# A hybrid decoder block on one core: the down projection's matmuls in two of 256 tokens

## The chip, the cores and the metric

The kernel runs on one core of a Trainium2 chip. The metric is the device time of one execution, in microseconds. Before the change two runs gave 2263.14 and 2269.77 us, median 2266.45 us.

## The reference, cut to what matters

One layer of a decoder on 512 tokens, model width 2048: a projection into three mixers (a state-space scan, a sparse attention and a short convolution), an output projection, and a gated MLP of width 5632. The change touches only the last product of the last lines, `@ ffn_w_down`:

```
h  = rmsnorm(x, norm_mix);  proj = h @ w_in
x  = x + concat[ssd(...), dsa(...), shortconv(...)] @ w_out
h2 = rmsnorm(x, norm_ffn)
g  = causal_dwconv(h2 @ ffn_w_gate, ffn_conv_w)      # 2048 -> 5632, 3 taps along the tokens
x  = x + (silu(g) * (h2 @ ffn_w_up)) @ ffn_w_down    # 5632 -> 2048
```

All is float32 at the interface. Inside, each operand of a large product is split in two, a rounded high part (type fp32r) and the rest as low part (fp32r too), and a product is made of three matmuls: high x high, low weights x high, high weights x low.

## The kernel before, in words

Everything is kept transposed: channels on the 128 partitions, the 512 tokens along the free axis. A weight tile is 128 x 128, a matmul takes it as its stationary operand (`whi` or `wlo`) and streams a 128 x 512 activation block (`hhi`, `yhi`, `ahi` or their low parts) into one bank of the accumulator memory, `ps`, which holds 512 float32 a partition.

Stages in time: the w_in projection with the mixers' work laid between its matmuls (to some 660 us), w_out (to some 825 us), then the MLP in 4 chunks of 11 feature tiles (1408 of the 5632 features). In a chunk, the gate and up projections fill `ahi`/`alo` (11 blocks of 128 x 512), and then the down projection, `down(ch)`, runs over the 16 output tiles: a hardware loop of 8 iterations with 2 output tiles each. One output tile contracts over the chunk's 11 feature tiles, in four quarters of 3, 3, 3 and 2 tiles (`DOWN_K`); its matmuls all add into one of two banks, and VectorE adds that bank to the residual (L1204).

The weights go through a chain of four engines, a quarter at a time: SyncE loads it from memory into one of 4 `raw` slots (L345), ScalarE rounds it into one of 8 `whi` slots (L636), GpSimd subtracts to get `wlo` (L376) and counts `lo_ready`, and TensorE waits for `lo_ready` at the head of the quarter (L400), runs the quarter's matmuls, and counts `w_used` with the last, which frees the slots. A tile's first quarter also waits until VectorE has read the bank, and each quarter waits for `a_lo`, the activations' low parts, which are early but for the last block in a chunk's first tile.

`quarter` is the function that issues a quarter's matmuls, for every projection: three a feature tile, lines 406, 407 and 408. For each matmul instruction that it issues, the trace shows two on TensorE, LDWEIGHTS (the engine PEld) and MATMUL (the engine PE). Down has 4 chunks x 16 output tiles x 11 feature tiles x 3 = 2112 matmuls. TensorE's other, smaller matmuls belong to the mixers (helper `side`); they are of plain float32, for which the trace shows two MATMULs an instruction, with a LDWEIGHTS each.

Of the kernel before, what the change touches and what calls it, by code (L numbers as in the profile page):

```python
# [29 lines left out]
T = 512  # L30
# [127 lines left out]
def hybrid_block(nc, xT, w_in, w_out, w_gu, w_dn, params, relb, cmats, onehot, bias_rows, acs_rows, out):  # L158
# [4 lines left out]
    with ExitStack() as ctx:  # L163
        def sb(name, shape, dt=F32):
            return ctx.enter_context(nc.sbuf_tensor(name, shape, dt))
# [9 lines left out]
        whi = sb("whi", [P, NW, T], F32R)  # L175
        wlo = sb("wlo", [P, NW, T], F32R)
# [93 lines left out]
        def bank(i):  # L270
            return ps[:, i, :]
# [67 lines left out]
        @block.sync  # L339
        def _(sp_):  # L340
            def load(slot, n, src, width):

                if not isinstance(n, int) or n >= NRAW:
                    sp_.wait_ge(lo_ready, n - NRAW + 1)
                sp_.dma_start(raw[:, slot % NRAW, 0:width], src).then_inc(raw_loaded[slot % NRAW], 16)  # L345


            for n in range(8):
                load(n, n, w_in[n % 2, :, n // 2 * T:(n // 2 + 1) * T], T)
                for i in {0: (0,), 1: (1,), 3: (2, 3), 5: (4, 5)}.get(n, ()):  # L350
                    load_x(sp_, i)
            load_x(sp_, 6)
            load_x(sp_, 7)
            with sp_.Fori(2, NPROJ) as t:
                for q in range(4):
                    load(q, 4 * t + q, w_in[bass.ds(t, 1), :, q * T:(q + 1) * T].rearrange("a p n -> (a p) n"), T)
            with sp_.Fori(0, KT) as t:
                for q in range(4):
                    load(q, 4 * t + (QN_OUT + q), w_out[bass.ds(t, 1), :, q * T:(q + 1) * T].rearrange("a p n -> (a p) n"), T)
            with sp_.Fori(0, FCH) as c:  # L360
                with sp_.Fori(0, 2 * FPC) as f:
                    for q in range(4):
                        load(q, QN_CHUNK * c + 4 * f + (QN_FFN + q),
                             w_gu[bass.ds(2 * FPC * c + f, 1), :, q * T:(q + 1) * T].rearrange("a p n -> (a p) n"), T)
                with sp_.Fori(0, KT) as d:
                    for q, (k0, kn) in enumerate(DOWN_K):
                        load(q, QN_CHUNK * c + 4 * d + (QN_FFN + 8 * FPC + q),
                             w_dn[bass.ds(KT * c + d, 1), :, k0 * P:(k0 + kn) * P].rearrange("a p n -> (a p) n"), kn * P)
# [26 lines left out]

        @block.tensor
        def _(pe):
            def quarter(slot, n, dst, src_hi, src_lo, ks, first, last, before=None):

                pe.wait_ge(lo_ready, n + 1)  # L400
                for i, k in enumerate(ks):
                    if before is not None:
                        before(k)
                    w = slice(i * P, (i + 1) * P)
                    s = slot % NW
                    nc.tensor.matmul(dst, whi[:, s, w], src_hi[:, k, :], start=first and i == 0, stop=False)  # L406
                    nc.tensor.matmul(dst, wlo[:, s, w], src_hi[:, k, :], start=False, stop=False)  # L407
                    ins = nc.tensor.matmul(dst, whi[:, s, w], src_lo[:, k, :], start=False,  # L408
                                           stop=last and i == len(ks) - 1)
                ins.then_inc(w_used, 1)  # L410
# [149 lines left out]
            for n in range(8):  # L560

                if n >= 4:
                    side(1, n - 4)
                quarter(n, n, acc(n % 2), hhi, hlo, range(4 * (n // 2), 4 * (n // 2) + 4), n < 2, n >= 6,
                        (lambda k: pe.wait_ge(h_lo, k + 1)) if n % 2 == 0 else None)
            for t in range(2, NPROJ):
                for q in range(4):
                    side(t, q)
                    if q == 0 and t >= 4:
                        wait_read(pe, t - 2)  # L570
                    quarter(4 * t + q, 4 * t + q, acc(t), hhi, hlo, range(4 * q, 4 * q + 4), q == 0, q == 3)


            for c in range(2):
                wait_read(pe, TN_OUT + c - 2)
                for q in range(4):
                    n = QN_OUT + 4 * c + q
                    quarter(n, n, bank((TN_OUT + c) % 2), yhi, ylo, range(4 * q, 4 * q + 4), q == 0, q == 3,
                            (lambda k: pe.wait_ge(y_lo, k + 1)) if c == 0 else None)
# [23 lines left out]
            def down(ch):  # L603
                with pe.Fori(0, KT // 2) as d:
                    for c in range(2):
                        pe.wait_ge(acc_read[(TN_FFN + c) % 2],
                                   (TN_CHUNK // 2) * ch + d + (TN_FFN + 2 * FPC + c - 2) // 2 + 1)
                        for q, (k0, kn) in enumerate(DOWN_K):

                            pe.wait_ge(a_lo, FPC * ch + (FPC if q == 3 else FPC - 1))  # L610
                            n = QN_FFN + 8 * FPC + 4 * c + q
                            quarter(n, QN_CHUNK * ch + 8 * d + n, bank((TN_FFN + c) % 2), ahi, alo,
                                    range(k0, k0 + kn), q == 0, q == 3)

            with pe.Fori(1, FPC) as f:
                for c in range(2):
                    gate_or_up(c, 8 * f, f)
            down(0)
            with pe.Fori(1, FCH) as ch:
                with pe.Fori(0, FPC) as f:  # L620
                    for c in range(2):
                        gate_or_up(c, QN_CHUNK * ch + 8 * f, (TN_CHUNK // 2) * ch + f)
                down(ch)
# [677 lines left out]
```

## Time and profile before

| | |
|---|---|
| runs shown | 2263.14 and 2269.77 us, median 2266.45 us |
| profiled execution | span 2264.7 us; the page gives no other time of it |
| TensorE matmuls (PE) | 2248.7 us busy (99%), 10196 |
| TensorE weight loads (PEld) | 1832.2 us busy (81%), 10196 |
| VectorE | 810.5 us (36%) |
| ScalarE | 754.0 us (33%) |
| GpSimd | 1076.2 us (48%) |
| DMA | mean 100 GB/s |

Busy time is time in which the engine had at least one instruction under way. A matmul's record lasts longer than the distance to the next one's, since they are pipelined, so a busy PE says little: the pace is read from the starts. The granted clock is given as a share of full speed, 1.00 for 2.4 GHz and 0.50 for 1.2 GHz.

### The profile page before, as it was taken

What the parts mean: (1) busy time and instruction counts of PE and PEld (TensorE: products, weight loads), DVE (VectorE), ACT (ScalarE), POOL (GpSimd) and SP (SyncE); (2) the same over time, 40 slices, a digit from 0 to 9 for tenths busy, and PEclk for the clock granted to TensorE, in tenths of its full rate; (3) what the DMA queues carried; (4) which work ended last, traced back from release to release, by engine and by line L of the source; (5) the groups of instructions that cost most, each with busy time, mean ns of one, the idle gap of its engine ahead of it and who ended that gap; (6) DMA issues with size and microseconds to landing.
All of it is one profiled execution on the core that took longest, in us unless ns stands there. A gap on an engine that the chain in (4) does not pass through costs nothing.

```text
span 2264.7 us, 32528 instructions
## 1 busy us (share of the span) xinstructions
PE 2248.7 (99%) x10196; PEld 1832.2 (81%) x10196; DVE 810.5 (36%) x1170; ACT 754.0 (33%) x1287; POOL 1076.2 (48%) x872
## 2 busy tenths in 40 slices
PE   8999999999999999999999999999999999999999
PEld 6777778887888888888888888888888888888887
DVE  5489565777651223222002233102233101332200
ACT  6343334443343334433222222222222222222221
POOL 4445334545464445444554444455444455444453
PEclk9999999999999999999999999999999999999999
DMA  5323122333252223222332222333222233222243
GB/s 185 87 81 117 63 70 86 121 96 99 83 186 96 96 82 111 94 96 85 96 112 94 99 96 89 91 96 109 97 97 97 80 98 110 96 97 93 86 132 97
DMA packets 132696, 226.18 MB, mean 100 GB/s; under 512 B 14728, under 2 KB 48968, under 8 KB 132648
## 3 DMA queue, kind: packets, MB, share of 16 engines
q1 hardware_dynamic: 126144, 210.82, 29.0%
q10 hardware_dynamic: 6504, 14.73, 2.0%
q8 instruction: 29, 0.48, 0.1%
q14 instruction: 19, 0.16, 0.0%
HBM read 220.74 MB, written 4.62 MB: 100 GB/s over the span
## 4 chain that ended last, share of the span: by engine, by line
PE 91%; DVE 6%; issue 1%; DMA 1%; ACT 1%; SPq 0%; ACTq 0%; DVEq 0%
PE ps L406 30%; PE ps L408 29%; PE ps L407 29%; DVE work L993 1%; DVE work L992 1%; DVE work L896 1%; PE ps L502 0%; PE ps L488 0%; DVE work L895 0%; DVE work L923 0%; PE ps L474 0%; DMA cm<-cmats 0%; DVE work L984 0%; PE ps L543 0%; DVE work L971 0%
## 5 line engine op out<-in xcount | busy, mean ns | idle before, releaser
L376 POOL TENSOR_TENSOR wlo<-raw,whi 128x512 fp32r<-128x512 f32 (+1 forms) x868 | 1076.0, 1246 | 1171.2 <-ACT whi L636 1170.3
L406 PE MATMUL ps<-hhi,whi 128*128 128x512 f32 x2192 | 867.8, 396 | 2.7 <-DVE hlo L1133 2.7
L408 PE MATMUL ps<-hlo,whi 128*128 128x512 f32 x2192 | 855.9, 390 | 0.0
L407 PE MATMUL ps<-hhi,wlo 128*128 128x512 f32 x2192 | 855.3, 390 | 0.0
L636 ACT ACTIVATE whi<-raw 128x512 fp32r<-128x512 f32 (+1 forms) x868 | 504.4, 589 | 931.6 <-PE ps L408 886.2
L406 PEld LDWEIGHTS ps<-hhi,whi 128*128 128x128 f32 x2192 | 412.7, 188 | 105.3 <-issue 17.9
L408 PEld LDWEIGHTS ps<-hlo,whi 128*128 128x128 f32 x2192 | 412.5, 188 | 87.2
L407 PEld LDWEIGHTS ps<-hhi,wlo 128*128 128x128 f32 x2192 | 413.0, 188 | 85.7 <-issue 2.4
L406 PE MATMUL ps<-ahi,whi 128*128 128x512 f32 x704 | 274.0, 389 | 0.0
L407 PE MATMUL ps<-ahi,wlo 128*128 128x512 f32 x704 | 274.0, 389 | 0.0
L408 PE MATMUL ps<-alo,whi 128*128 128x512 f32 x704 | 273.9, 389 | 0.0
L1204 DVE TENSOR_TENSOR resid<-ps,resid 128x512 f32 x64 | 44.3, 692 | 424.1 <-PE ps L408 424.1
L407 PEld LDWEIGHTS ps<-ahi,wlo 128*128 128x128 f32 x704 | 132.2, 188 | 27.5
L406 PEld LDWEIGHTS ps<-ahi,whi 128*128 128x128 f32 x704 | 132.2, 188 | 27.4
L408 PEld LDWEIGHTS ps<-alo,whi 128*128 128x128 f32 x704 | 132.2, 188 | 27.3
L1194 DVE TENSOR_TENSOR upv<-ps,rstd 128x512 f32<-128x512 f32 x44 | 30.4, 691 | 295.0 <-PE ps L408 295.0
L1185 DVE TENSOR_TENSOR gpad<-ps,rstd 128x512 f32<-128x512 f32 x44 | 30.5, 692 | 294.7 <-PE ps L408 294.2
L407 PE MATMUL ps<-yhi,wlo 128*128 128x512 f32 x256 | 99.6, 389 | 0.0
L408 PE MATMUL ps<-ylo,whi 128*128 128x512 f32 x256 | 99.6, 389 | 0.0
L406 PE MATMUL ps<-yhi,whi 128*128 128x512 f32 x256 | 99.6, 389 | 0.0
L836 ACT ACTIVATE gsilu<-gconv 128x512 f32<-128x512 f32 x44 | 27.8, 632 | 139.6 <-DVE gconv L1189 139.6
L1197 DVE TENSOR_TENSOR act<-upv,gsilu 128x512 f32<-128x512 f32 x44 | 69.0, 1569 | 8.7 <-DVE upv L1194 8.7
(171 smaller groups left out, 1215.0 us busy)
## 6 DMA issues: line engine op xcount, KB each, us to landing
raw<-w_gu SPq DMA_DIRECT2D x352, 256.0 KB, 3.1
raw<-w_in SPq DMA_DIRECT2D x196, 256.0 KB, 3.2
raw<-w_dn SPq DMA_DIRECT2D x192, 192.0 KB, 2.3
raw<-w_out SPq DMA_DIRECT2D x64, 256.0 KB, 3.1
raw<-w_dn SPq DMA_DIRECT2D x64, 128.0 KB, 2.2
resid<-xT SPq DMA_DIRECT2D x8, 512.0 KB, 7.1
work<-acs_rows ACTq DMA_DIRECT2D x8, 512.0 KB, 3.9
resid<-xT ACTq DMA_DIRECT2D x8, 512.0 KB, 7.2
```

What stands on the lines that cost most here:

```text
L376: nc.gpsimd.tensor_tensor(wlo[:, slot % NW, 0:width], raw[:, slot % NRAW, 0:width], whi[:, slot % NW, 0:width].bitcast(F32), ALU.subtract) ...
L406: nc.tensor.matmul(dst, whi[:, s, w], src_hi[:, k, :], start=first and i == 0, stop=False)
L407: nc.tensor.matmul(dst, wlo[:, s, w], src_hi[:, k, :], start=False, stop=False)
L408: ins = nc.tensor.matmul(dst, whi[:, s, w], src_lo[:, k, :], start=False, stop=last and i == len(ks) - 1)
L636: A(whi[:, slot % NW, 0:width], raw[:, slot % NRAW, 0:width], ACT.Copy).then_inc(hi_ready, 1)
L836: A(gsilu[:, :], gconv[:, :], ACT.Silu).then_inc(f_silu, 1)
L896: ch_.link(V.scalar_tensor_tensor(r, t, 1.5, r, ALU.add, ALU.mult))
L992: ch_.link(V.max(top8, score[b]))
L1185: V.tensor_tensor(gpad[:, 2:], bank(TN_FFN % 2), rstd2[:, :], ALU.mult).then_inc(acc_read[TN_FFN % 2], 1)
L1194: V.tensor_tensor(upv[:, :], bank(par1), rstd2[:, :], ALU.mult).then_inc(acc_read[par1], 1)
L1197: V.tensor_tensor(act[:, :], upv[:, :], gsilu[:, :], ALU.mult).then_inc(f_act, 1)
L1204: V.tensor_tensor(blk(resid, 2 * d + p), bank((TN_FFN + p) % 2), blk(resid, 2 * d + p), ALU.add).then_inc(acc_read[(TN_FFN + p) % 2], 1)
```

## The change

`quarter` gets a flag, `halves`, which is set in `down` alone. With it, each matmul of 128 x 512 becomes two of 128 x 256, with the same weights, one directly behind the other: tokens 0 to 255 and tokens 256 to 511, into the two halves of the same bank. The flag that starts the bank's sum anew stands at the first half of the tile's first matmul alone. The count `w_used` goes with the last half.

```diff
-            def quarter(slot, n, dst, src_hi, src_lo, ks, first, last, before=None):
+            def quarter(slot, n, dst, src_hi, src_lo, ks, first, last, before=None, halves=False):
...
                     s = slot % NW
+                    if halves:
+                        for weight, src in ((whi, src_hi), (wlo, src_hi), (whi, src_lo)):
+                            for h in range(2):
+                                cols = slice(h * T // 2, (h + 1) * T // 2)
+                                ins = nc.tensor.matmul(dst[:, cols], weight[:, s, w], src[:, k, cols],
+                                                       start=first and i == 0 and weight is whi and src is src_hi and h == 0,
+                                                       stop=last and i == len(ks) - 1 and src is src_lo,
+                                                       skip_group_check=True)
+                        continue
...
                             quarter(n, QN_CHUNK * ch + 8 * d + n, bank((TN_FFN + c) % 2), ahi, alo,
-                                    range(k0, k0 + kn), q == 0, q == 3)
+                                    range(k0, k0 + kn), q == 0, q == 3, halves=True)
```

TensorE's program before, in `down`: the head of a quarter and two of its feature tiles (the `REGISTER_ALU` row computes the value of a wait):

```order
L400 REGISTER_ALU [waits a_lo]
L406 MATMUL ps<-ahi,whi 128x512 [waits lo_ready]
L407 MATMUL ps<-ahi,wlo 128x512
L408 MATMUL ps<-alo,whi 128x512
L406 MATMUL ps<-ahi,whi 128x512
L407 MATMUL ps<-ahi,wlo 128x512
L408 MATMUL ps<-alo,whi 128x512
```

And in the changed kernel, the same place (`x2` counts two instructions alike in a row; the first of a quarter stands apart because it carries the wait):

```order
L400 REGISTER_ALU [waits a_lo]
L410 MATMUL ps<-ahi,whi 128x256 [waits lo_ready]
L410 MATMUL ps<-ahi,whi 128x256
L410 MATMUL ps<-ahi,wlo 128x256 x2
L410 MATMUL ps<-alo,whi 128x256 x2
L410 MATMUL ps<-ahi,whi 128x256 x2
L410 MATMUL ps<-ahi,wlo 128x256 x2
```

Nothing has moved: every matmul stands in its old place, twice and half as wide, and the waits sit where they sat. The other engines' programs are the same.

## Rows read from the trace of the kernel before

**Rows 1.** The page: the span and the busy time of the engines.
```profile
span 2264.7 us, 32528 instructions
PE 2248.7 (99%) x10196; PEld 1832.2 (81%) x10196; DVE 810.5 (36%) x1170; ACT 754.0 (33%) x1287; POOL 1076.2 (48%) x872
PE 91%; DVE 6%; issue 1%; DMA 1%; ACT 1%; SPq 0%; ACTq 0%; DVEq 0%
```

**Rows 2.** Timeline of PE (start us, duration us), down's first matmul of chunk 1, and the next after its last.
```profile
1064.37 0.39 PE L406 MATMUL ps<-ahi,whi 128*128 128x512 f32 x1
...
1184.05 0.39 PE L406 MATMUL ps<-hhi,whi 128*128 128x512 f32 x1
```

**Rows 3.** Windows: stretch, busy us and count by engine (PE, PEld, DVE, ACT, POOL), clock, DMA.
```profile
12.00:17.00 5.00, 5.00 (x14) 3.84 (x13) 4.61 (x5) 4.75 (x9) 2.94 (x2) 0.50 0.97 333
414.00:416.00 2.00, 2.00 (x31) 1.58 (x29) 0.69 (x1) 0.74 (x2) 0.00 (x0) 1.00 0.40 129
588.00:596.00 8.00, 8.00 (x59) 6.59 (x58) 3.53 (x9) 1.27 (x3) 6.40 (x5) 1.00 0.58 163
1064.00:1184.00 120.00, 120.00 (x531) 99.40 (x530) 12.71 (x18) 33.28 (x65) 61.94 (x64) 1.00 0.34 101
```

**Rows 4.** Timeline of PE at the half clock, twelve matmuls: the first and the last.
```profile
11.86 0.63 PE L407 MATMUL ps<-hhi,wlo 128*128 128x512 f32 x1
...
16.55 0.63 PE L406 MATMUL ps<-hhi,whi 128*128 128x512 f32 x1
```

**Rows 5.** Timeline of PEld, the weight loads around six float32 matmuls of 128 columns.
```profile
410.91 0.19 PEld L529 LDWEIGHTS ps<-work 128*128 128x128 f32 x1
411.47 0.19 PEld L406 LDWEIGHTS ps<-hhi,whi 128*128 128x128 f32 x1
411.58 0.19 PEld L407 LDWEIGHTS ps<-hhi,wlo 128*128 128x128 f32 x1
```

**Rows 6.** Timeline of PE: float32 matmuls of 128 and of 512 columns.
```profile
410.91 0.83 PE L529 MATMUL ps<-work 128*128 128x128 f32 x6
...
95.25 1.02 PE L441 MATMUL ps<-work,cm 128*128 128x512 f32 x2
```

**Rows 7.** Groups by line: the means of down's matmuls and loads, and of L441's.
```profile
L406 PE MATMUL ps<-ahi,whi 128*128 128x512 f32 x704 | 274.0, 389 | 0.0
L441 PE MATMUL ps<-work,cm 128*128 128x512 f32 x16 | 8.3, 597 | 0.2 <-ACT work L652 0.2
L406 PEld LDWEIGHTS ps<-ahi,whi 128*128 128x128 f32 x704 | 132.2, 188 | 27.4
```

**Rows 8.** Timeline of PE behind a burst of small matmuls: nine matmuls, first and last.
```profile
416.44 0.39 PE L407 MATMUL ps<-hhi,wlo 128*128 128x512 f32 x1
...
418.30 0.39 PE L406 MATMUL ps<-hhi,whi 128*128 128x512 f32 x1
```

**Rows 9.** Who waited for whom, us in total, times, longest us.
```profile
POOL wlo L376 <- ACT whi L636: 1170.3, 713, 14.3
ACT whi L636 <- PE ps L408: 886.2, 573, 3.1
DVE resid L1204 <- PE ps L408: 424.1, 64, 6.8
```

**Rows 10.** Timeline: the last `alo`, the quarter that waits for it, the kernel's last sum.
```profile
1067.30 0.69 DVE L1200 TENSOR_TENSOR alo<-act,ahi 128x512 f32 x1 [0.89 <-ACT ahi L841]
...
1070.49 0.39 PE L406 MATMUL ps<-ahi,whi 128*128 128x512 f32 x1
...
2260.94 0.39 PE L408 MATMUL ps<-alo,whi 128*128 128x512 f32 x1
2261.49 0.69 DVE L1204 TENSOR_TENSOR resid<-ps,resid 128x512 f32 x1 [6.79 <-PE ps L408]
```

**Rows 11.** DMA queues of the whole span: the instructions' own.
```profile
q8 instruction: 29, 0.48, 0.1%
```

## The prediction, made before the changed kernel had run

> **What bounds the kernel now.** I read the page first. TensorE is busy in 99% of the span, and the chain of waits lies on it for 91% [rows 1]. The reader should see that this says who sets the end, and not how fast it goes, because a matmul's record (389 ns) is longer than the distance to the next one.
>
> So the next view is the timeline of PE around the stage that the change touches. The first matmul of `down` in chunk 1 starts at 1064.37 us, and the first matmul behind its last at 1184.05 [rows 2]. Between them lie 4 x 4 x 11 x 3 = 528 matmuls, 16 output tiles of 33: 119.68 us / 528 = **226.7 ns** from start to start. The windows show TensorE without a gap there and at a granted clock of 1.00 (2.4 GHz), while ScalarE works 33.3, GpSimd 61.9 and VectorE 12.7 us of 120 [rows 3]. Nothing but TensorE's own pace sets this stage. The waits say the same from the other side: the weight chain waits for TensorE (ScalarE 886 us, for `w_used`), as does VectorE's sum (424 us), and GpSimd waits for ScalarE, which waits for TensorE [rows 9]. The four `down` stages are 4 x 119.7 = 479 us, 21% of the span. A gain or a loss in TensorE's pace there reaches the end in full, and nothing else does.
>
> The one question is then what 256 columns cost beside 512, with a weight load for each.
>
> **The pace, taken apart.** At the half clock, eleven distances between matmuls of 512 columns come to 16.55 - 11.86 = 4.69 us, 426 ns each [rows 4], at a granted 0.50 [rows 3]. That is one column a cycle with nothing added. Twice the clock would give 213.2 ns, and the row says 226.7: at full speed, **13.5 ns** are added to each matmul. They are the whole matter. Either they are added once an instruction (a start of the stream, a disturbance by the weight load), and the change pays them twice, or they come with the columns (a source that gives 16 columns in the time of 17), and the change pays nothing.
>
> The plain float32 rows show how little a start can cost. L441's two MATMULs are busy for 1.02 us with a mean of 0.597 for one, so the second starts 0.42 us behind the first [rows 6, 7]; a float32 MATMUL of 512 columns streams for 2 x 213.2 = 426 ns, so nothing to speak of is added.
>
> **The change, part by part.**
>
> *The weight loads.* 2112 are added, one for each added matmul; nothing in the diff removes the second. Today a load (record 188 ns [rows 7]) lies under a stream of 213 ns. Behind the change it lies under one of half that. What a load needs at least is in the trace: at 410.91 us a burst of six float32 matmuls of 128 columns starts its second load, and five loads later L406's starts at 411.47, and then L407's at 411.58 [rows 5]: 560 / 5 = 112, and 110 ns. Each of these matmuls streams for 106.6 ns, as long as a fp32r matmul of 256 columns, and has its load of 128 x 128 with a record of the same length. So loads and streams of just this size are shown to alternate at **112 ns**. It is the floor of a half: 2 x 112 = 224 ns a pair against 226.7, which is -2.7 x 2112 = -5.7 us. The loads alone don't make the stage slower, but nothing of today's slack is left.
>
> The Trainium skill ("TensorE: Matmul & The Clock Gate", section LDWEIGHTS) gives a load as columns / 1.2, 107 ns for 128; the trace's 110 to 112 from load to load agree.
>
> *The streams.* A half is 106.6 ns of columns and some of the 13.5. The bounds: with none of it, the floor of 112; with its share by columns, 113.3, so 226.7 a pair and **0 us**; with all of it, 106.6 + 13.5 = 120.1, so 240.2 a pair, +13.5 x 2112 = **+28.5 us**. Above that stands what the trace shows behind bursts: from 416.44 to 418.30 us eight distances take 1.86 us, 232.5 ns each at full clock [rows 8], 5.8 more than in the steady stream. If halves ran like that throughout, a half would be 120.1 + 5.8 = 125.9, and the sum 2 x 125.9 - 226.7 = 25.1 x 2112 = +53.0 us.
>
> I take the 13.5 as a cost of the instruction. For it speaks that the pace is not the same wherever the columns are the same (226.7 and 232.5), so something at the boundary between instructions moves it; a pure rate would not know of a burst before it. Against it speaks that the float32 rows have boundaries too and add next to nothing, though they ask for a column only every second cycle and may hide it.
>
> *Order, banks, waits.* The halves write to different columns of the bank, and the next matmul on the same columns comes one later, as long behind in time as before. The flag that starts the sum anew stays at one a tile. The waits stand in their places: nothing is queued behind a new one. The last `alo` block of the chunk is ready at 1067.30 + 0.69 = 1067.99, its quarter starts at 1070.49 [rows 10]: 2.5 us of cover, and more if the quarters get longer. 0 us.
>
> *The other engines* get no instruction. A longer stage gives them more slack: GpSimd has 61.9 us of work in 120. 0 us. The end: VectorE's last sum starts 0.55 us behind the start of the last matmul [rows 10]; with a half in its place, 0.1 us less. 0 us.
>
> *The program* grows by 66 matmuls and loads in each of two copies of the loop. TensorE's and the others' instructions come in 29 packets in the whole span, 0.1% of the DMA engines [rows 11]; one or two more hide in it.
>
> **Sum.** +28.5 us on a span of 2264.7. The median of the runs, 2266.45, lies 1.75 us above the span, which I carry over: 2266.45 + 28.5 = **2295 us**, +1.3%.
>
> **The rivals.** About 2%, 45 us either way, is what a measurement of this kernel can tell from no change.
>
> *The added time goes with the columns (0.29).* A pair costs 226.7, or a few ns more because a load of 112 ns under a stream of 113.3 leaves no room for a late one: 0 to +4 ns a pair, 2266 to 2275 us. For it: the steady pace is very even: 531 records in the window of 120 us [rows 3], which 226.7 ns a matmul would give (120 / 0.2267 = 529, and the two that reach in). Against it: rows 8.
>
> *The floor holds, or less (0.04).* 112 ns a half gives 2266.45 - 5.7 = 2261 us. If the loads overlapped better than these rows show, the halves could come at their 106.6 ns: 2 x 106.6 = 213.2, -13.5 x 2112 = 2238 us. No row has it.
>
> The same skill page (section Back-to-back issue gap) has a matmul at columns / 2.4 + 2.5 ns, so 109 for a half, 218 a pair and 2248 us by it; at 512 columns it says 216, where this trace has 226.7, so I don't follow it.
>
> *Instructions aren't delivered fast enough (0.08).* This is the case on the other side. The place is TensorE's sequencer in `down`'s loop: it issues one load and one matmul in 226.7 ns now, and needs two of each. The densest long stretch, 8 us, has 59 matmuls and 58 loads, 68.4 ns an instruction [rows 3]. If this were its limit, a pair would cost 4 x 68.4 = 273.6, +46.9 x 2112 = +99 us: 2365. It decides from (226.7 + 21.3) / 4 = 62 ns an instruction, where the sum passes 2%. Against it: a stretch of 2 us has 31 and 29, 33 ns each [rows 3], and L406 goes on behind it without idle time; but a queue that had filled before can feed 2 us.
>
> The skill's page on TensorE (Part 2: What happens when you issue a matmul, "Decode and dispatch") gives 62 ns a matmul for a sequencer that decodes in software; if loads cost the same that is 248 a pair and 2311 us. No run here shows which way this chip decodes.
>
> *Halves in the state behind a burst (0.05).* 2266.45 + 53.0 = 2319 us, as priced above.
>
> *The change doesn't do what it says (0.04).* If the second load were dropped when the program is built or run, its count would stay near 10196 and the second half would follow without a boundary: 2266 us. Today's trace has a load for each matmul, 10196 of both, but hardly two matmuls in a row with the same weights to show it.
>
> **How the numbers follow.** Forecast 0.50 (2288 to 2302), by columns 0.29, floor 0.04, delivery 0.08, behind-a-burst state 0.05, second load dropped 0.04. Over 2% faster (below 2221): only what overlaps beyond all rows, 0.01. Over 2% slower (above 2312): 0.08 + 0.05, less 0.01 for a burst state that holds only in part, 0.12. The rest, 0.87, is within 2%. The range must hold both large cases: from 2262, under the case by columns, to 2306, eleven above the forecast for some of the state behind bursts. It leaves out 0.04 + 0.12 and the edges of the forecast. The likeliest case alone has 2288 to 2302.
>
> **What would show it.** The page should count 12308 matmuls and as many loads. The gate and up projections must keep 226.7 ns. In `down` I look for the distance between starts: 120 and 120 by the forecast, 113 and 113 by columns, 112 at the floor, 126 and more in the last cases; uneven distances, short within a pair and long between pairs, would say that the same weights matter after all. If delivery were the limit, PE's row would show gaps with the releaser "issue". The stage should last 4 x 33 x 4 pairs at the pair's price, 126.8 us instead of 119.7. I am wrong most likely in the one place where I chose without a row: whether the 13.5 ns belong to the instruction or to the columns.

## The result, and the profile after

The changed kernel took 2297.6 us (median of two runs, 2296.59 and 2298.61). Its ratio to the kernel before is **1.0136, interval 1.0099 to 1.0173**: 1.4% slower, a little more than was forecast (2295.0 us). The profiled execution took 2298.61 us with a span of 2296.8.

The page after, its first lines and the groups of `down` (answers to [rows 1] and [rows 7]; in a group busy us, mean ns of one, idle us before it):

```profile
span 2296.8 us, 36752 instructions
PE 2276.4 (99%) x12308; PEld 1941.0 (85%) x12308; DVE 813.1 (35%) x1170; ACT 753.5 (33%) x1287; POOL 1076.0 (47%) x872
...
L410 PE MATMUL ps<-ahi,wlo 128*128 128x256 f32 x1408 | 283.7, 283 | 0.0
...
L410 PEld LDWEIGHTS ps<-ahi,whi 128*128 128x128 f32 x1408 | 219.9, 192 | 0.3
```

There are 12308 matmuls and as many loads, 2112 more of each, so the second load of a pair is not dropped. The share of PE is 99% as before: it tells nothing of the loss. PE had no idle time before a half.

The timeline of PE after, first matmul of `down` in chunk 1, and the next behind its last (answers to [rows 2]):

```profile
1068.27 0.40 PE L410 MATMUL ps<-ahi,whi 128*128 128x256 f32 x2
...
1194.98 0.40 PE L415 MATMUL ps<-hhi,whi 128*128 128x512 f32 x1
```

126.71 us for 1056 halves is **120.0 ns** from start to start, 240.0 a pair; before it was 226.7. Inside, the pairs follow evenly, and so do their loads (timelines of PE and of PEld, start us and duration us; `x2` is one row for a pair):

```profile
1071.86 0.40 PE L410 MATMUL ps<-ahi,whi 128*128 128x256 f32 x2
1072.10 0.40 PE L410 MATMUL ps<-ahi,wlo 128*128 128x256 f32 x2
1072.34 0.40 PE L410 MATMUL ps<-alo,whi 128*128 128x256 f32 x2
```

```profile
1071.98 0.31 PEld L410 LDWEIGHTS ps<-ahi,wlo 128*128 128x128 f32 x2
1072.22 0.31 PEld L410 LDWEIGHTS ps<-alo,whi 128*128 128x128 f32 x2
```

The four `down` stages grew by 7.03 us each, 28.1 together, and the span by 32.1. The remaining 4 us lie elsewhere. Windows of the mixers' stretch, of the kernel before, of the changed one, and of a second profile of the changed one (the first experiment):

```profile
200.00:440.00 240.00, 238.91 (x1249) 186.57 (x1249) 150.33 (x332) 89.79 (x188) 99.69 (x71) 1.00 0.26 87
440.00:640.00 200.00, 197.23 (x1024) 161.35 (x1021) 144.87 (x162) 82.55 (x121) 106.99 (x66) 1.00 0.31 99
```

```profile
200.00:440.00 240.00, 237.74 (x1236) 185.65 (x1235) 150.90 (x331) 89.81 (x188) 99.25 (x71) 1.00 0.26 86
440.00:640.00 200.00, 196.12 (x1018) 160.14 (x1017) 145.91 (x160) 80.80 (x117) 103.78 (x64) 0.99 0.30 96
```

```profile
200.00:440.00 240.00, 238.93 (x1255) 186.54 (x1255) 150.07 (x332) 90.08 (x189) 99.28 (x71) 1.00 0.26 86
440.00:640.00 200.00, 197.24 (x1020) 161.24 (x1015) 145.08 (x161) 82.69 (x121) 107.23 (x67) 1.00 0.31 99
```

TensorE is idle 1.2 and 1.1 us more in these two stretches in the one profile, and no more than before in the other, of the same program. Its first half starts at 1068.27 us in the one and at 1063.99 in the other, against 1064.37 before. Of the 3.9 us by which the first one is later than before, 2.3 are this idle time and 1.6 a slower clock. Before a burst of the mixers (L538, L529 in the kernel before) TensorE waits 2.26 us instead of 1.14, because one VectorE instruction ahead of it (L905) took 1.83 us and not 0.69; behind this wait the granted clock falls to the half for some matmuls, which then follow each other at 0.43 us. The burst in the timeline of PE, in the kernel before and in the changed one (in brackets the wait ahead of it), and a window of the changed one behind it, with a mean clock of 0.55:

```profile
513.57 0.94 PE L529 MATMUL ps<-work 128*128 128x128 f32 x6 [1.14 <-DVE work L1078]
```

```profile
515.87 1.40 PE L538 MATMUL ps<-work 128*128 128x128 f32 x6 [2.26 <-DVE work L1087]
```

```profile
515.80:519.30 3.50, 3.43 (x12) 2.95 (x13) 1.34 (x6) 0.00 (x0) 0.00 (x0) 0.55 0.31 107
```

The same fall of the clock, between 510 and 521 us, stands in the traces of the experiments 3, 5, 6, 7 and 8 below, and not in those of 1, 2, 4 and 9 to 12. So the 4 us are not the change's; they come in some executions, hundreds of us ahead of the first half. They also mean that the total of a single run can be off by a few us, and that the stage is the better measure.

The waits after (engine, line, whom it waited for: us, times, longest us):

```profile
POOL wlo L376 <- ACT whi L645: 1201.2, 713, 14.3
ACT whi L645 <- PE ps L417: 558.7, 330, 4.3
DVE resid L1213 <- PE ps L410: 452.3, 64, 7.2
ACT whi L645 <- PE ps L410: 357.4, 244, 1.8
```

All follow TensorE as in [rows 9]: the weight chain's two waits make 916 us (886 before), VectorE's 452 (424). The loss is TensorE's own pace, and the others wait longer for it.

### The profile page after: what moved, and what is told of

It is laid out like the page before. It is cut to its first block, busy times and chain, and to the rows that moved or that the text cites. A ratio compares the mean times of both kernels' runs of the same rounds, so it can differ in the third digit from the quotient of the medians.

```text
span 2296.8 us, 36752 instructions
## 1 busy us (share of the span) xinstructions
PE 2276.4 (99%) x12308; PEld 1941.0 (85%) x12308; DVE 813.1 (35%) x1170; ACT 753.5 (33%) x1287; POOL 1076.0 (47%) x872
## 4 chain that ended last, share of the span: by engine, by line
PE 91%; DVE 6%; issue 1%; DMA 1%; ACT 1%; SPq 0%; ACTq 0%; DVEq 0%
PE ps L415 22%; PE ps L410 22%; PE ps L417 22%; PE ps L416 22%; DVE work L1002 1%; DVE work L1001 1%; DVE work L905 1%; PE ps L511 0%; PE ps L497 0%; DVE work L932 0%; DVE work L904 0%; PE ps L483 0%; DMA cm<-cmats 0%; DVE work L993 0%; PE ps L552 0%
## 5 line engine op out<-in xcount | busy, mean ns | idle before, releaser
L410 PE MATMUL ps<-ahi,wlo 128*128 128x256 f32 x1408 | 283.7, 283 | 0.0
L410 PE MATMUL ps<-alo,whi 128*128 128x256 f32 x1408 | 283.7, 283 | 0.0
L410 PE MATMUL ps<-ahi,whi 128*128 128x256 f32 x1408 | 283.7, 283 | 0.0
L410 PEld LDWEIGHTS ps<-ahi,whi 128*128 128x128 f32 x1408 | 219.9, 192 | 0.3
L410 PEld LDWEIGHTS ps<-alo,whi 128*128 128x128 f32 x1408 | 219.6, 192 | 0.0
L410 PEld LDWEIGHTS ps<-ahi,wlo 128*128 128x128 f32 x1408 | 219.6, 192 | 0.0
```

The source lines that it names most:

```text
L410: ins = nc.tensor.matmul(dst[:, cols], weight[:, s, w], src[:, k, cols], start=first and i == 0 and weight is whi and src is src_hi and h ...
```

## The experiments

The theories. **S**: the added time (13.5 ns in the prediction, 13.3 from here on, since 512 columns at 2.4 GHz are 213.3 ns) is a start, paid once an instruction, whatever is loaded. **By columns**: it comes with the columns. **L** came up on the way: it comes from the weight load beneath the stream, in proportion to its width. **U** stands in the last run's expectation, after a whole matmul with a narrow load had turned out uneven: whole matmuls with any load narrower than 128 columns cost about 230 ns, while halves follow L. All experiments touch the matmuls of `down` alone, unless said, and are built from the changed or the old kernel. The stage in `down` is the instrument: its first start, and that of the next stage's first matmul, over the count. Times of a single run are given without an interval.

### 1. The changed kernel again

> The changed kernel itself, timed again beside the kernel before, as the measure for the others. Theory S (start): every fp32r matmul costs its columns at 2.4 GHz and 13.3 ns once, so a half takes 120.0 ns from start to start and the four down stages last 28.2 us longer; I expect a ratio of 1.0124 (28.2 of 2266), 1.010 to 1.015. What the first profile showed above 28.2 us lay in the mixers' stretch, which the change doesn't touch: it should be there in some runs of either kernel and not in others. If it belongs to the change, the ratio is 1.014 again.

Measured: 2295.02 us (2293.65 to 2298.37, four runs) against 2267.01, ratio **1.0126, interval 1.0107 to 1.0145**; the stage takes 126.713 us, 120.0 ns a half. This is the better figure for the change: +28.0 us, of which the four stages hold 28.1.

### 2. The halves apart

```diff
-for weight, src in (...):
-    for h in range(2):
+for h in range(2):
+    for weight, src in (...):
```

> The same 4224 half matmuls, but the three of the first 256 tokens come before the three of the others, so no matmul has the weights of the one before it. Theory S: nothing changes, 120.0 ns each, 28 us above the kernel before. Rival N (neighbours): equal weights one behind the other are treated specially (cheaper, or dearer because the same weights are read twice at once); then this kernel's pace is not 120 in down.

Measured: 2292.52 us. The timeline of PE:

```profile
1062.21 0.28 PE L410 MATMUL ps<-ahi,whi 128*128 128x256 f32 x1
1062.32 0.28 PE L410 MATMUL ps<-ahi,wlo 128*128 128x256 f32 x1
...
1188.92 0.40 PE L415 MATMUL ps<-hhi,whi 128*128 128x512 f32 x1
```

126.71 us again, 120.0 ns. That a half has the same weights as the one before it, or the same columns of the bank, makes no difference.

### 3. 384 and 128 columns

```diff
-    for h in range(2):
+    for lo_, hi_ in ((0, 384), (384, 512)):
```

> Each matmul of down as one of 384 and one of 128 columns. Theory S with the floor of the weight load (112 ns from load to load, as the plain float32 burst of before has it): 384 columns take 160 + 13.3 = 173.3 ns, 128 columns would take 53.3 + 13.3 = 66.7 but wait for the next load, 112: 285 a pair, 58.6 x 2112 = 124 us above the kernel before. Rival without a floor (loads are taken ahead further than one matmul): 240 a pair, +28 us, with distances of 173 and 67.

Measured: 2396.94 us. From 1068.09 to 1219.39 us there are 528 pairs:

```profile
1068.09 0.33 PE L410 MATMUL ps<-ahi,whi 128*128 128x384 f32 x1
...
1219.39 0.45 PE L415 MATMUL ps<-hhi,whi 128*128 128x512 f32 x1
```

286.6 ns a pair, where 285 was expected and 240 is what equal halves take. The starts of the records alternate by 229 and 58 ns, and 58 ns is less than any distance between two loads in this stage, so a 384 is recorded to start before its load can be there; the loads' distances, 179 and 108, are nearer to the turn that was expected, 173 under the long stream and 112 under the short one, but no record shows that split itself. What is shown is the pair: without a floor it would take 240 ns, and it takes 286.6. The expectation's reading fits: a piece of 128 columns does not cost its 53 + 13 = 67 ns but the 112 of the next load. An uneven split costs 59.9 ns a pair, where the even one costs 13.3. (The four stages hold 126.5 us of the 129.9 that the run is longer; the clock's fall described above is in this trace.)

### 4. Four pieces of 128 columns

```diff
-    for h in range(2):
+    for lo_, hi_ in ((0, 128), (128, 256), (256, 384), (384, 512)):
```

> Each matmul of down as four of 128 columns. Theory S with the floor: 112 ns each whatever the stream needs, 448 for the four, 221 x 2112 = +467 us. Without the floor: 4 x 66.7 = 267, +84 us. If the sequencer's delivery has a limit near 68 ns an instruction (the densest long stretch of before), the pace would be 137 ns, 547 for the four, +676 us, and PE would show idle time released by issue.

Measured: 2729.89 us. Timeline ends of the stage, and a group by form (x count: ns min/median/max, first and last start):

```profile
1062.12 0.56 PE L410 MATMUL ps<-ahi,whi 128*128 128x128 f32 x4
...
1297.91 0.45 PE L415 MATMUL ps<-hhi,whi 128*128 128x512 f32 x1
```

```profile
L410 PEld LDWEIGHTS ps<-ahi,wlo x2816: 191/192/193, 1062.5 to 2723.1; 128*128 128x128 f32 x188
```

235.79 us / 2112 = **111.6 ns** each, the floor that [rows 5] gave as 110 to 112. It also settles the rival of delivery: 111.6 ns for a load and a matmul is 56 ns an instruction, kept up for 236 us, below the 68.4 that the rival took and the 62 from which it would decide.

The Trainium skill ("TensorE: Matmul & The Clock Gate", Part 2, "Decode and dispatch") has 62 ns a matmul. With a load priced the same a pair of instructions would take 124 ns; the run has 111.6, so the figure is no limit here in that reading; run 6 below has a matmul every 60.0 ns, each with its load, which is under 62 even for the matmul alone.

### 5 and 6. Narrow loads: 512 and 128 columns with 64 weight columns

The loads take 64 of the 128 weight columns, and the matmuls fill 64 rows of the bank: half of the output is left out. The number of columns streamed is the same.

```diff
-    matmul(dst[:, cols], weight[:, s, w], ...)
+    matmul(dst[0:64, cols], weight[:, s, i * P:i * P + 64], ...)
```

> Whole matmuls of 512 columns in down as in the kernel before, but each loads and multiplies only 64 of the 128 weight columns: the upper half of every down output is left out. It halves the weight load. Theory S (start): the 13.3 ns belong to the start of the stream, and the pace stays 226.7 ns, the time that of the kernel before. Theory L (load): the 13.3 ns are what the load of 128 weight columns takes from the stream beside it; half a load takes half, 220.0 ns a matmul, -14 us in down.

> Each matmul of down as four of 128 columns, again with 64 of the 128 weight columns (the upper half of every down output is left out). The load of 64 columns should need about half of 111.6, 56 to 58 ns, less than what the stream needs. Theory S: 53.3 + 13.3 = 66.7 ns each, 267 for the four, 40 x 2112 = +84 us above the kernel before. Theory L: 53.3 + 6.7 = 60.0, 240 for the four, +28 us. If the load's floor doesn't depend on its width: 111.6 again, +464 us.

Measured, 512 columns: 2278.41 us; the stage lasts from 1069.23 to 1190.67 us:

```profile
1075.21 0.39 PE L410 MATMUL ps<-alo,whi 128*64 128x512 f32 x1
1075.44 0.39 PE L410 MATMUL ps<-ahi,whi 128*64 128x512 f32 x1
1075.67 0.40 PE L410 MATMUL ps<-ahi,wlo 128*64 128x512 f32 x1
...
1190.67 0.39 PE L415 MATMUL ps<-hhi,whi 128*128 128x512 f32 x1
```

230.0 ns each, in a repeated pattern of six (236, 229, 225, 226, 234, 230 ns). That is neither S (226.7) nor L (220): a narrower load makes the whole matmul **slower**. (3.3 x 2112 = 7 us of the 12 that this run is longer; the rest lies ahead of the first stage, which starts at 1069.23 us.) Measured, 128 columns: 2293.54 us, 126.7 us / 2112 = 60.0 ns, L's number, where S had 66.7:

```profile
1062.84 0.28 PE L410 MATMUL ps<-ahi,whi 128*64 128x128 f32 x2
...
1189.56 0.45 PE L415 MATMUL ps<-hhi,whi 128*128 128x512 f32 x1
```

60 is near what a load of 64 weight columns needs, if 112 ns are needed for 128, so this one could be the floor instead. The two contradict each other under either theory. Run 6 also settles delivery better than run 4 does: a load and a matmul in 60.0 ns are 30 ns an instruction, kept up for 126.7 us.

### 7 and 8. `down` in bfloat16, whole and in halves

The high and low parts of `down`'s operands are rounded to bfloat16 and hold fewer bits; the kernel is otherwise the same (the weight chain writes to tiles `whb` and `wlb` of that type).

```diff
-ahi, alo = ... F32R
+ahi, alo = ... bfloat16
+whb, wlb = ... bfloat16          # for whi, wlo in down
...
-(whi, src_hi), (wlo, src_hi), (whi, src_lo)
+(whb, src_hi), (wlb, src_hi), (whb, src_lo)
```

> Down's operands (both parts of the activations and of the weights) in bfloat16 instead of fp32r, three matmuls of 512 columns as in the kernel before; high and low parts then hold fewer bits. Theory S in its narrower form (the 13.3 ns are a start that only a stream of 4-byte elements at one column a cycle can't hide, as plain float32 at one column in two cycles hides it): the pace is that of float32 rows, columns + 2, 215.3 ns, so 11.3 x 2112 = 24 us less than the kernel before, 2243 us. If the start belongs to any full-rate stream: 226.7 and no change.

> The same in bfloat16, each matmul in two of 256 columns. Narrow form of S: 106.7 + 2 = 108.7 ns each unless the load's floor of 111.6 holds for bfloat16 weights too; 217 or 223 a pair, -20 or -8 us against the kernel before. If the start belongs to any full-rate stream: 120.0 each, +28 us.

Measured, whole: 2244.12 us against 2266.47, ratio **0.9897, interval 0.988 to 0.9913**. In this trace the record of each output tile's first matmul is missing, so the pace is read from the stage's second matmul to its last, 526 distances in 113.53 us:

```profile
1065.27 0.38 PE L415 MATMUL ps<-ahi,wlb 128*128 128x512 bf16 x1
...
1178.80 0.38 PE L415 MATMUL ps<-alo,whb 128*128 128x512 bf16 x1
```

That is **215.8 ns**, which run 11 confirms without a gap (113.96 us / 528). Halves: 2250.14 us, 115.21 us / 1056 = 109.1 ns, 218.2 a pair. That is below the 111.6 of run 4, so that floor is not one of bfloat16 loads. The groups, of whole ones and of halves:

```profile
L415 PE MATMUL ps<-ahi,wlb 128*128 128x512 bf16 x704 | 266.8, 379 | 1.8
...
L415 PEld LDWEIGHTS ps<-ahi,whb 128*128 128x128 bf16 x704 | 68.9, 98 | 83.6 <-issue 1.0
```

```profile
L415 PE MATMUL ps<-ahi,whb 128*128 128x256 bf16 x1408 | 268.9, 273 | 0.0
...
L415 PEld LDWEIGHTS ps<-ahi,wlb 128*128 128x128 bf16 x1408 | 137.8, 98 | 15.8
```

At the same columns and the same count, bfloat16 adds 2.5 ns to an instruction at 512 columns and 2.4 at 256, where fp32r adds 13.3 at both. So the 13.3 are not a start that any matmul has. Whether they go with the type of the stream or with that of the load is not separated: these runs change both, and the bfloat16 load is another one too. It is recorded with 98 ns and not 188 to 192, and the trace gives its source as 32 x 1 x 4 elements where fp32r has 128 x 1 x 1. In bfloat16 the same split costs 2.4 ns a pair, some 5 us, under a fifth of what it costs here.

The Trainium skill ("TensorE: Matmul & The Clock Gate", Back-to-back issue gap) has columns / 2.4 + 2.5 ns, 109 for 256 and 216 for 512. It gives this for single matmuls, without the loads between them. The bfloat16 runs, which have a load for each, agree to 1 ns. It does not carry over to fp32r, which has 120.0 and 226.7.

### 9. Narrow loads in halves

As 5, with 256 columns a matmul; half of the output is left out.

> The halves of 256 columns with only 64 of the 128 weight columns loaded and multiplied (the upper half of every down output is left out). The two runs with narrow loads before it disagree: whole matmuls took 230.0 ns (theory L had 220, S 226.7), pieces of 128 columns 60.0 ns (L's number; S had 66.7). Here neither the load's floor (about 58 for 64 columns) nor four loads a matmul stand in the way. Theory S (a start of 13.3 ns an instruction, whatever the load): 120.0 ns. Theory L (what the load takes from the stream goes with the load's columns): 113.3 ns. If the uneven pace of the whole matmuls (224 to 236 ns) comes from narrow loads as such, both get some 3 ns more.

Measured: 2264.49 us (before: 2266.35). Timeline ends:

```profile
1062.26 0.40 PE L410 MATMUL ps<-ahi,whi 128*64 128x256 f32 x2
1062.49 0.39 PE L410 MATMUL ps<-ahi,wlo 128*64 128x256 f32 x2
...
1181.94 0.40 PE L415 MATMUL ps<-hhi,whi 128*128 128x512 f32 x1
```

119.687 us / 1056 = **113.3 ns**, evenly 113 and 114. No floor is near here (half of 112 is 56), and S, with 120.0, falls: with as many instructions of as many columns, halving the load halves what is added, 13.3 to 6.7 ns.

### 10. 384 columns alone

128 of the 512 tokens are left out of `down`.

```diff
-    for h in range(2):
-        cols = slice(h * T // 2, (h + 1) * T // 2)
+    for h in range(1):
+        cols = slice(0, 384)
```

> Each matmul of down on the first 384 tokens alone, one matmul with its full load in place of two halves (the down projection of tokens 384 to 511 is left out). Both S and L: 160 + 13.3 = 173.3 ns, so the cost stays the same at a width between 256 and 512. A cost by columns after all, of which 256 and 512 would be two points by chance, has 13.3 x 384/512 = 10.0: 170.0 ns.

Measured: 2151.35 us, 91.546 us / 528 = **173.4 ns**, that is 160.0 of columns and 13.4:

```profile
1061.64 0.33 PE L410 MATMUL ps<-ahi,whi 128*128 128x384 f32 x1
...
1153.19 0.39 PE L415 MATMUL ps<-hhi,whi 128*128 128x512 f32 x1
```

By columns it would be 170.0. With 512, 384 and 256 columns the addition is 13.3, 13.4 and 13.3 ns: it does not go with the columns at all.

### 11. bfloat16 from the output projection on

The largest thing that 7 points to: the three products with `w_out`, gate, up and `down`, 7104 matmuls, with parts of bfloat16 (fewer bits in the high and low parts); only `w_in` keeps fp32r.

```diff
-hhi, hlo, yhi, ylo, ahi, alo: F32R
+hhb, hlb, yhi, ylo, ahi, alo: bfloat16
...
+wh, wl = (whi, wlo) if src_hi is hhi else (whb, wlb)
```

> The kernel before with bfloat16 parts instead of fp32r in every product from w_out on: w_out, gate, up and down, 768 + 4224 + 2112 = 7104 matmuls of 512 columns. If each goes from 226.7 to the 215.1 ns that down showed in bfloat16, it is 11.6 x 7104 = 82 us less than the kernel before, 2184 us, ratio 0.964, and the fastest of all. If the weight chain (ScalarE, GpSimd) or the DMA were near its limit in gate and up, part of it would come back as a wait for lo_ready.

Measured: 2190.16 us (2186.43 to 2190.68, four runs) against 2266.35, ratio **0.9662, interval 0.9646 to 0.9679**. That is 76 us less, where 82 was expected; the expectation took 215.1 ns a matmul, and with the 215.8 of run 7 it is 10.8 x 7104 = 77 us. It is the fastest kernel of this study that does the whole work, with less precision in the parts:

```profile
span 2187.9 us, 32542 instructions
...
L415 PE MATMUL ps<-hhb,whb 128*128 128x512 bf16 x1408 | 533.6, 379 | 0.0
```

### 12. More widths of load

First chunk: 32 weight columns and halves of 256. Others: 512 columns, with 96 weight columns for one output tile and 32 for the other. From a quarter to three quarters of the output is left out.

```diff
-    matmul(dst[:, cols], weight[:, s, w], ...)
+    matmul(dst[0:m, cols], weight[:, s, i * P:i * P + m], ...)    # m = 32 or 96
```

> Three load widths in one kernel; the rest of each down output is left out. In the first chunk's down: halves of 256 columns with 32 weight columns. In the other three: whole matmuls of 512 columns, with 96 weight columns for the first of the two output tiles in the loop and 32 for the second. Theory L, as 128 and 64 weight columns have it at 256 (120.0 and 113.3 ns): 13.33 x width / 128 on top of the stream, so 106.7 + 3.3 = 110.0 ns for the halves, 213.3 + 10.0 = 223.3 and 213.3 + 3.3 = 216.7 ns for the whole ones. Theory U (only whole matmuls with narrow loads are uneven, as the 230.0 ns at 64 columns): the halves follow L at 110.0, the whole ones stay between 224 and 236 ns, with a mean near 230.

Measured: 2278.53 us. The first chunk, and the others' first:

```profile
1065.36 0.40 PE L411 MATMUL ps<-ahi,whi 128*32 128x256 f32 x2
...
1189.73 0.40 PE L416 MATMUL ps<-hhi,whi 128*128 128x512 f32 x1
...
1429.12 0.39 PE L411 MATMUL ps<-ahi,whi 128*96 128x512 f32 x1
...
1550.90 0.39 PE L416 MATMUL ps<-hhi,whi 128*128 128x512 f32 x1
```

124.37 us / 1056 = 117.8 ns with 32 weight columns, where L has 110.0: a load of a quarter adds 11.1 ns, more than one of half. The whole ones take 121.78 us / 528 = 230.6 ns, a mean of 230.0 with 96 and of 231.3 with 32. The whole ones run as U has it, but U too had 110.0 for the halves. **L falls too** as a law, at 256 columns with the loads of 32. What was added in all fp32r cases, in ns an instruction (the distance less columns / 2.4):

| weight columns | 128 streamed | 256 | 384 | 512 |
|---|---|---|---|---|
| 128 | load's floor, 111.6 in all | 13.3 | 13.4 | 13.3 |
| 96 | | | | 16.6 |
| 64 | 6.7 (may be the floor) | 6.7 | | 16.7 |
| 32 | | 11.1 | | 18.0 |

## Why the prediction was right

**What bounds the kernel.** Right. The stage grew by exactly its matmuls, and nothing else in the program moved with it: between `down` stages the gate and up projections keep their pace (443 matmuls from 1250 to 1350 us in both kernels), and every wait still ends at TensorE.

**The weight loads.** Right: 2112 more, none dropped, and they alone do not slow the stage. The floor of 112 ns, read from five loads around a burst [rows 5], was measured at 111.6 over 2112 in a row (run 4). A half at 120.0 stands 8 ns above it.

**The streams.** This was the step on which all hung, and the one taken without a row: that the 13.5 ns belong to the instruction. A half was put at 106.6 + 13.5 = 120.1 and takes 120.0; the sum was +28.5 us and the stages grew by 28.1. Run 10 confirms it at a third size, 173.4 ns at 384 columns, where the case by columns wanted 170.0. The choice was right, but the reason given for it was weaker than the outcome suggests: the chances stated were 0.50 against 0.29, no row decided between the two, and that this choice came out was in part luck. I argued from the slower pace behind a burst [rows 8] that "something at the boundary between instructions" moves it. No run looked at that pace again. The runs show a cost that is paid once an instruction and yet is no plain start: bfloat16 pays 2.5 ns (runs 7 and 8), and halves with half a weight load pay 6.7 (run 9). What the prediction named as "a disturbance by the weight load" beside the start is the nearer of its two readings, though no run has a matmul without its load, so what the stream and what the load add can't be told apart. I also set the float32 rows aside as perhaps hiding it; nothing here tests that.

**Order, banks, waits.** Right at 0: apart or together, the halves cost the same (run 2).

**The end.** Before, the last sum started 0.55 us behind the last matmul [rows 10]; now the last half starts 0.12 us behind 2293.04 and the sum at 2293.60, 0.44 us, the 0.1 us less that was named.

```profile
2293.04 0.40 PE L410 MATMUL ps<-alo,whi 128*128 128x256 f32 x2
2293.60 0.69 DVE L1213 TENSOR_TENSOR resid<-ps,resid 128x512 f32 x1 [7.22 <-PE ps L410]
```

**The program.** Its own DMA went from 29 packets to 30:

```profile
q8 instruction: 30, 0.49, 0.1%
```

**The size.** The first median lies 2.6 us above the forecast; its profiled execution has 4 us in the mixers' stretch that are not the change's, a longer wait and a fall of the clock. The four runs of run 1 have a median of 2295.02 us, the forecast.

**The rivals.** By columns: fell (120.0 and not 113.3; 173.4 and not 170.0). That a kernel with 113.3 ns a half exists at all (run 9) shows what its time would have been: 2264 us, the 2266 worked out. Floor: it exists at 111.6, where pieces of 128 columns meet it, and halves stay above it. Delivery: fell, 30 ns an instruction are kept up (run 6). Behind a burst, 126 ns a half: does not occur in the changed kernel. Second load dropped: fell.

**What stays open.** What the 13.3 ns are. Shown: fp32r has them and bfloat16, with its own kind of load, has 2.5; each instruction with its load of 128 weight columns pays them, whatever the columns streamed; and the width of the load changes them. Not separated: the type of the stream and the type of the load; a matmul of one with the load of the other was not run. Not shown: the law. With 256 streamed, 128, 64 and 32 weight columns add 13.3, 6.7 and 11.1; with 512 streamed, narrower loads make it worse, and uneven, 224 to 236 ns, much like the 232.5 behind a burst. When in a stream a load begins and ends might decide, but no run moved that alone.

## What to carry to other kernels

Compare the distance between matmul starts with columns over the clock; what is left over is paid per matmul and load, so measure it at two sizes before splitting, and for the type in use. Splitting a matmul pays it again (13.3 ns in fp32r, some 2.5 in bfloat16), and a piece of 128 columns costs the 112 ns from load to load instead (run 4, fp32r). A kernel that is bound so gains from a type with a smaller remainder, where its precision allows (3.4% here), and not from taking its halves apart (run 2).

## What was not expected of the hardware

- At full clock, the same instruction stream with fewer weight columns can be slower: 230.0 ns with 64 against 226.7 with 128, both with 512 streamed.
- A MATMUL's recorded start can stand before the load that it needs is done: the 384s of run 3 are recorded 58 ns behind the 128s, and no two of the loads are nearer than 107. Distances over a long stretch hold, single ones do not.
- A load in bfloat16 is recorded with 98 ns and in fp32r with 188 to 192, at the same 128 x 128; in fp32r the records are 162, 134 and 108 ns for 96, 64 and 32 weight columns (runs 12, 5 and 12).
